# Gates and branch projections with tokens on partitions in a two-layer transformer kernel

## The chip, the cores and the metric

The kernel runs on one core of one Trainium2 chip. Its time is the device time in microseconds (us) of one execution. Beside it stands the span of a profiled execution, which runs from its first to its last instruction.

## The reference, cut to what matters

Two blocks follow one another on 256 tokens of width 2048. Each has a mixer and a feed-forward part. What the change touches is the mixer's gates, its two branch projections and the out projection behind them:

```
z = u @ w_in                                  # u: rms-normed input, 256 x 2048
... , gates = split(z)                        # the last 4096 columns of z
y_a = (first branch: a scan in layer 1, a gated MLP in layer 2)      # 256 x 1024
y_b = (second branch: banded / neighbourhood attention)              # 256 x 1024
gate_a, gate_b = split(sigmoid(gates))        # 256 x 2048 each
merged = gate_a * (y_a @ w_branch_a) + gate_b * (y_b @ w_branch_b)
h = h + merged @ w_out
```

All of it is float32. Layer 2 does the same with `w_in_2`, `w_branch_2` (both halves in one matrix) and `w_out_2`.

## The kernel before, in words

**Products.** Each weight is split into a high and a low float32r part, and so is each operand (`XU` and `XY` hold 16 tiles of 128 features; columns 0 to 255 of a tile are the high parts of the 256 tokens, 256 to 511 the low parts). A product is high*high + high*low + low*high. In `products` the weights are stationary: for each of 8 contraction tiles k of a block, `high(k)` (L432) holds 128x128 of `w_hi` and streams 512 columns of X, and `low(k)` (L437) holds `w_lo` and streams 256. The result has output features on partitions and tokens in the free dimension. In `value_products` and `token_downs` the other layout is used: 128 tokens of X are stationary and 512 columns of a weight chunk stream, three matmuls (L469, L470, L471) for each of two token halves; the result has tokens on partitions.

**The weight stream.** All weights come in blocks of 512 KB in the order in which they are used, by SP, into five slots. ACT rounds block b+4 to `w_hi` (`round_block`, L799), DVE subtracts to get `w_lo` (`low_part`, L1216), and PE multiplies block b. ACT rounds a block only when PE has finished the block that held its slot five blocks earlier (`w_used`). Every engine runs its own straight program in block order, so an ACT step of block b can stand behind a wait for PE's block b.

**The stages in order**, for layer 1: `vals1` (values, tokens on partitions), `heads1` (8 heads of 18 blocks), `branch1` (32 blocks), `out1` (32 blocks), then the feed-forward stages; for layer 2: `gmv`, `heads2` (8 heads of 14 blocks), `branch2`, `out2`, feed-forward. In a head, the first 5 tiles (3 in layer 2) are inputs of the scan or the attention; the last 4 tiles, 8 blocks, are gate columns. A tile takes two blocks (16 contraction tiles). Between blocks PE does small jobs of the scan and the attention (lists `after1`, `after2`). The last jobs of a head in layer 1 stand behind block 17: `attend` (L598, L603) and `scan_rms` (L567).

**What ACT does around the end of a head in layer 1** (step b = 17, then step b = 0 of the next head): it copies the cross half of a finished tile (`copy_cross`, L804), rounds a block, copies the attention's high part (L900), takes Ln and Exp of the scan's norm (L940, L941), waits for two DVE products, copies the result (L943), and then rounds the next block. The next head's step b = 1 has `sigmoid_of` (L880). In layer 2, step b = 0 rounds a block, which needs PE to have finished block 0 of this head, and step b = 1 has a Gelu (L1081).

**Banks.** In `heads1` tile t uses `acc_first` for t = 0 and else `acc[(t-1) % 2]`; in `heads2` the two `acc` banks in turn. A gate tile is summed on DVE (`tile_sum`: bank plus cross), multiplied by `rs` and kept in `G` (L1407, L1580). In the branch stages ACT takes the sigmoid in `G` (L956), and DVE multiplies, adds and forms the low part of the mixed tile (L1436 to L1441), one 128x256 tile at a time, so that the out projection's operand is there with features on partitions.

Of the kernel before, what the change touches and what calls it, by code (L numbers as in the profile page):

```python
# [6 lines left out]
F32 = mybir.dt.float32  # L7
# [32 lines left out]
CHUNK = 512  # L40
OUT_ACT = 3 * D // 8
# [103 lines left out]

def phases():
    plan = [("vals1", 1, 32, 0, 0, None), ("heads1", HEADS, 18, 9, 9, None), ("branch1", 2, 16, 16, 16, None), ("out1", 2, 16, 8, 0, None),
# [3 lines left out]
            ("gmv", 1, 32, 0, 0, None), ("heads2", HEADS, 14, 7, 7, None),  # L151
            ("branch2", 2, 16, 16, 16, None), ("out2", 2, 16, 8, 0, None),
# [21 lines left out]
def two_blocks(  # L174
# [6 lines left out]
    with ExitStack() as ctx:  # L181
# [70 lines left out]
        def head2_bank(i, t):  # L252
            return acc[(7 * i + t) % 2]
# [58 lines left out]
        def gate_of(i, b):  # L312

            j, half = divmod(b, 2)
            return i * 16 + (4 * (j // 2) + 2 * half + j % 2)

        def mixed_before(b, blocks):

            return [b // 2 - 1] if b and b % 2 == 0 else [b // 2] if b == blocks - 1 else []
# [36 lines left out]
        def _(sp):  # L356
# [13 lines left out]
            def side(name, i, b):  # L370
# [6 lines left out]
                if name == "ffn1last" and b == 0:  # L377
# [5 lines left out]
                    sp.wait_ge(S("mz_ready1"), KD)  # L383
                    sp.dma_start(Gf[:, 0:2 * WIDTH],
                                 bass.AP(tensor=norm_rows.tensor, offset=0, ap=[[0, P], [1, 2 * WIDTH]])).then_inc(S("bs_in"), 16)
                if name == "ffn2first" and b == 0:
                    sp.wait_ge(S("mz_ready2"), KD)
                    sp.dma_start(final_row, bass.AP(tensor=norm_rows.tensor, offset=2 * WIDTH, ap=[[0, P], [1, D]])).then_inc(S("bs_in"), 16)
# [30 lines left out]
        def _(pe):  # L419
# [53 lines left out]

            def raw_products(b, banks):
# [49 lines left out]
            def in_tiles(p, i, X, after, bank_of):  # L524
                for b in range(p.blocks):
                    t = b // 2
                    if b % 2 == 0:
                        bank_free(p, i, t)
                    if i == 0 and b in (0, 2):

                        pe.wait_ge(S("vals_out" if p.name == "heads1" else "av_out"), NT * (1 + 2 * (p.name == "heads1") + b // 2))
                    products(p, i, b, bank_of(t), X, KB * (b % 2), b % 2 == 0, b % 2 == 1)
                    for job in after.get(b, []):
                        job(i)
# [91 lines left out]
            for i in range(p.iters):  # L626
                in_tiles(p, i, XU, after1, lambda t: acc_first if t == 0 else acc[(t - 1) % 2])

            def branches(name):

                p = ph[name]
                X = XY if name == "branch1" else XU
                x = name[-1]
                for i in range(p.iters):
                    for b in range(p.blocks):
                        pe.wait_ge(acc_free, p.tile(i, b) - 3 + TILE_CREDIT)
                        if b < 2:

                            pe.wait_ge(acc_free, p.tbase - 1 + b + TILE_CREDIT)
                        if i + b == 0:  # L640

                            pe.wait_ge(S(f"ya_ready{x}"), HEADS - 1)
                            products(p, i, b, four_banks[0], X, 0, True, True, ks=range(KB - 1), used=0)
                        elif i == 0 and b == 1:
                            pe.wait_ge(S(f"yb_ready{x}"), HEADS)
                            products(p, i, b, four_banks[1], X, KB, True, True, used=0)
                            pe.wait_ge(S(f"ya_ready{x}"), HEADS)
                            products(p, i, 0, four_banks[0], X, 0, True, True, ks=(KB - 1,), used=2)
                        else:
                            products(p, i, b, four_banks[b % 4], X, KB * (b % 2), True, True)  # L650

            def out_projection(name):
                p = ph[name]
                X = XU if name == "out1" else XY
                for i in range(p.iters):
                    for b in range(p.blocks):
                        if b % 2 == 0:
                            bank_free(p, i, b // 2)
                        products(p, i, b, acc[b // 2 % 2], X, KB * (b % 2), b % 2 == 0, b % 2 == 1,
                                 operand=one_by_one(S(f"m_ready{name[-1]}"), 0) if b < 2 else None)  # L660
# [103 lines left out]
            for i in range(p.iters):  # L764
                in_tiles(p, i, XY, after2, lambda t: head2_bank(i, t))
# [18 lines left out]
        def _(act):  # L784
# [92 lines left out]

            def sigmoid_of(n, wait_name, done_name, i):
# [24 lines left out]
            for i in range(p.iters):  # L903
                for b in range(p.blocks):
                    t = b // 2
                    if b == 0:
                        round_next(p, i, b)
                    if b % 2:

                        copy_cross(p, i, t, b, acc_first if t == 0 else acc[(t - 1) % 2])  # L910
# [37 lines left out]

            def branches(name, X):
                p, x = ph[name], name[-1]  # L950
                act.wait_ge(S(f"gates_z{x}"), HEADS)
                for i in range(p.iters):
                    for b in range(p.blocks):
                        round_block(p, i, b)
                        gate = G[:, ds(gate_of(i, b), 1), :]
                        act.activation(gate, gate, ACT.Sigmoid).then_inc(S(f"gates_ready{x}"), 1)  # L956
                        free_cross(p, i, b)
                        copy_cross(p, i, b, b, four_banks[b % 4])

                        for j in mixed_before(b, p.blocks):  # L960
                            act.wait_ge(S(f"mz_ready{x}"), i * 8 + j + 1)
                            act.activation(X[:, ds(i * 8 + j, 1), 0:T], work[:, 2 * (j % 2):2 * (j % 2) + 1, 0:T], ACT.Copy)\
                               .then_inc(S(f"mh_ready{x}"), 1)
# [8 lines left out]
            def out_projection(name, X, n0, c0):  # L972
                p = ph[name]
                for i in range(p.iters):
                    for b in range(p.blocks):
                        round_block(p, i, b)
                        if b % 2:
                            j = i * 8 + b // 2
                            operand_tile(n0 * KD + j, X, j, cols[:, ds(j + c0, 1)], p, i, b // 2)
# [3 lines left out]
            out_projection("out1", XY, 0, C_MLP1)  # L983
# [89 lines left out]
            for i in range(p.iters):  # L1073
                for b in range(p.blocks):
                    t = b // 2
                    if b % 2:
                        copy_cross(p, i, t, b, head2_bank(i, t))
                    round_next(p, i, b)
                    if b == 1:
# [16 lines left out]
            out_projection("out2", XU, 2, C_FFN2)  # L1096
# [67 lines left out]
        def _(pool):  # L1164
# [12 lines left out]
            def out_projection(name, n0):  # L1177
                p = ph[name]
                for i in range(p.iters):
                    for b in range(p.blocks):  # L1180
                        if b % 2:
                            add_square(i * 8 + (n0 * KD + b // 2))
# [18 lines left out]
        def _(dve):  # L1201
# [157 lines left out]
            for i in range(p.iters):  # L1359
                for b in range(p.blocks):  # L1360
# [10 lines left out]
                    bank = acc_first if t == 0 else acc[(t - 1) % 2]  # L1371
# [32 lines left out]
                    if b in (11, 13, 15, 17):  # L1404
                        n = (b - 11) // 2
                        tile_sum(p, i, 5 + n, b, 5 + n, bank, wk(8))
                        ins = V.tensor_tensor(G[:, ds(i * 4 + n, 1), :], work[:, 8:9, 0:T],  # L1407
                                              rs[:, :].rearrange("p (a t) -> p a t", a=1), ALU.mult)
                        if n == 3:
                            mark(ins, S("gates_z1"), i + 1)  # L1410
                        else:
                            link(ins)
# [11 lines left out]

            def branches(name, X):
                p, x = ph[name], name[-1]
                for i in range(p.iters):
                    for b in range(p.blocks):
                        low_part(p, i, b)
                        j, half = divmod(b, 2)  # L1430
                        at = 2 * (j % 2)
                        z = work[:, at + half:at + half + 1, 0:T]
# [343 lines left out]
```

## Time and profile before

| | us |
|---|---|
| median of 3 runs | 2780.59 |
| lowest and highest | 2780.02, 2781.06 |
| the profiled execution, its own time | 2781.22 |
| its span | 2779.4 |

The profiled execution's own time is 1.8 us more than its span, and 0.6 us above the median of the runs. Starts in a timeline are us from the start of the span. PE is TensorE's matmuls, PEld its weight loads, which overlap the matmuls. The recorded end of a matmul is modelled and overlaps the next one, so rates are read from starts.

### The profile page before, as it was taken

Reading aid. Unit: us, or ns where it says so; the run is one execution under the profiler, and the core shown is the slowest. Engines: PE = TensorE matmul, PEld = TensorE weight load, DVE = VectorE, ACT = ScalarE, POOL = GpSimd, SP = SyncE. Lnnn points to the kernel's source line nnn. Section 1 sums busy time; section 2 is a strip of 40 time slices with the busy share of each in tenths; the row PEclk is TensorE's granted clock in tenths of the full one; section 3 lists DMA queues with packets and bytes.
Section 4 is the critical chain, followed back from the end, with each engine's and each line's share of the span. In section 5 each row is a group of like instructions: output and inputs, shape, how many; then the busy total and the mean of one; then the engine's idle time right before and its main releaser. Section 6 shows DMA issues by size and latency. Waiting matters only on the chain.

```text
span 2779.4 us, 40598 instructions
## 1 busy us (share of the span) xinstructions
PE 2765.6 (100%) x15440; PEld 2377.4 (86%) x15440; DVE 2075.5 (75%) x3194; ACT 1472.1 (53%) x2184; POOL 63.6 (2%) x72
## 2 busy tenths in 40 slices
PE   9999999999999999999999999999999999999998
PEld 6888888888888888888888888888888888888887
DVE  5687888887677777777786677778778777777776
ACT  5456555565444444444465555556555555555554
POOL 0000000000000000000050000000000000000000
PEclk9999999999999999999999999999999999999999
DMA  7555555555555655555655655655565555555554
GB/s 266 189 172 166 187 173 174 172 190 189 181 193 190 193 184 189 190 191 188 210 197 188 195 180 169 196 175 188 184 203 190 183 192 191 192 190 190 190 189 144
DMA packets 157154, 521.98 MB, mean 188 GB/s; under 512 B 28960, under 2 KB 31392, under 8 KB 156704
## 3 DMA queue, kind: packets, MB, share of 16 engines
q1 hardware_dynamic: 155952, 517.31, 56.5%
q8 instruction: 123, 2.02, 0.3%
q10 hardware_dynamic: 1008, 2.08, 0.2%
q14 instruction: 71, 0.58, 0.1%
HBM read 517.22 MB, written 2.10 MB: 187 GB/s over the span
## 4 chain that ended last, share of the span: by engine, by line
PE 100%; DMA 0%; DVE 0%; ACT 0%; issue 0%; DVEq 0%; SPq 0%
PE acc L432 39%; PE acc L437 19%; PE psT L432 5%; PE psX L432 5%; PE acc_first L432 5%; PE psX L437 3%; PE psT L437 3%; PE acc_first L437 2%; PE acc L469 1%; PE acc L471 1%; PE acc L470 1%; PE psT L715 1%; PE psE L715 1%; PE psE L716 1%; PE psX L717 1%; PE psA L717 1%
## 5 line engine op out<-in xcount | busy, mean ns | idle before, releaser
L1216 DVE TENSOR_TENSOR w_lo<-w_raw,w_hi 128x1024 fp32r<-128x1024 f32 x958 | 1170.3, 1228 | 344.5 <-ACT w_hi L799 315.4
L799 ACT ACTIVATE w_hi<-w_raw 128x1024 fp32r<-128x1024 f32 x958 | 1003.0, 1055 | 553.0 <-PE acc L432 280.3
L432 PE MATMUL acc<-XU,w_hi 128*128 128x512 f32 x2848 | 930.6, 398 | 0.0
L437 PEld LDWEIGHTS acc<-XU,w_lo 128*128 128x128 f32 x2848 | 535.3, 188 | 122.5
L432 PE MATMUL acc<-XY,w_hi 128*128 128x512 f32 x1792 | 576.8, 397 | 0.0
L437 PE MATMUL acc<-XU,w_lo 128*128 128x256 f32 x2848 | 560.0, 278 | 0.0
L432 PEld LDWEIGHTS acc<-XU,w_hi 128*128 128x128 f32 x2848 | 447.8, 189 | 4.1 <-issue 2.7
L437 PEld LDWEIGHTS acc<-XY,w_lo 128*128 128x128 f32 x1792 | 336.7, 188 | 78.3
L437 PE MATMUL acc<-XY,w_lo 128*128 128x256 f32 x1792 | 352.4, 278 | 0.0
L432 PEld LDWEIGHTS acc<-XY,w_hi 128*128 128x128 f32 x1792 | 277.9, 189 | 5.5 <-DVE work L1222 2.7
L804 ACT ACTIVATE cross<-acc 128x256 f32<-128x256 f32 x242 | 92.5, 382 | 335.2 <-PE acc L432 335.2
L432 PE MATMUL acc_first<-XU,w_hi 128*128 128x512 f32 x576 | 188.0, 398 | 0.0
L1222 DVE TENSOR_TENSOR work<-acc,cross 128x256 f32<-128x256 f32 x242 | 102.5, 424 | 105.8 <-ACT cross L804 104.2
L437 PEld LDWEIGHTS acc_first<-XU,w_lo 128*128 128x128 f32 x576 | 108.2, 188 | 25.3
L437 PE MATMUL acc_first<-XU,w_lo 128*128 128x256 f32 x576 | 113.3, 278 | 0.0
L432 PE MATMUL psX<-XU,w_hi 128*128 128x512 f32 x320 | 107.0, 395 | 0.0
L432 PE MATMUL psT<-XU,w_hi 128*128 128x512 f32 x320 | 107.0, 395 | 0.0
L432 PE MATMUL psT<-XY,w_hi 128*128 128x512 f32 x320 | 104.4, 395 | 0.0
L432 PE MATMUL psX<-XY,w_hi 128*128 128x512 f32 x320 | 104.4, 395 | 0.0
L432 PEld LDWEIGHTS acc_first<-XU,w_hi 128*128 128x128 f32 x576 | 90.4, 189 | 0.7
L1167 POOL TENSOR_TENSOR sqacc<-sqacc,sqb 128x256 f32<-128x256 f32 x48 | 43.7, 910 | 1941.0 <-ACT sqb L969 1940.5
L1003 ACT ACTIVATE XU<-work 128x256 fp32r<-128x256 f32 x64 | 26.7, 418 | 98.9 <-DVE work L1482 98.9
(345 smaller groups left out, 3275.9 us busy)
## 6 DMA issues: line engine op xcount, KB each, us to landing
w_raw<-in_weights SPq DMA_DIRECT2D x962, 512.0 KB, 3.4
bias<-in_rel_bias SPq DMA_DIRECT2D x8, 384.0 KB, 3.9
bias<-in_rpb_back SPq DMA_DIRECT2D x32, 96.0 KB, 6.7
hT<-in_x_t SPq DMA_DIRECT2D x8, 256.0 KB, 7.5
G<-in_norm_rows SPq DMA_DIRECT2D x2, 1024.0 KB, 7.3
G<-in_pair_masks ACTq DMA_DIRECT2D x1, 960.0 KB, 5.1
out_dram<-G SPq DMA_DIRECT2D x2, 384.0 KB, 2.5
out_dram<-G ACTq DMA_DIRECT2D x2, 384.0 KB, 3.2
```

Of the source, the lines that this page charges most:

```text
L432: return nc.tensor.matmul(bank[:, :], hi[:, k, col:col + P], X[:, k0 + k, :], start=first and k == 0, stop=last and k == nk - 1 and k % 2 ...
L437: return nc.tensor.matmul(bank[:, 0:T], lo[:, k, col:col + P], X[:, k0 + k, 0:T], start=False, stop=last and k == nk - 1 and k % 2 == 0, s ...
L469: nc.tensor.matmul(bank[:, :], x_hi, hi[:, k, :], start=first, stop=False, skip_group_check=True)
L470: nc.tensor.matmul(bank[:, :], x_hi, lo[:, k, :], start=False, stop=False, skip_group_check=True)
L471: done = nc.tensor.matmul(bank[:, :], x_lo, hi[:, k, :], start=False, stop=last, skip_group_check=True)
L715: nc.tensor.matmul(bank[:, :], x_hi, hi[:, e, :], start=k == 0 and s.group >= 0, stop=False, skip_group_check=True)
L717: done = nc.tensor.matmul(bank[:, :], x_lo, hi[:, e, :], start=False, stop=k == nk - 1, skip_group_check=True)
L799: act.activation(w_hi[s][:, 0:n], w_raw[s][:, 0:n], ACT.Copy).then_inc(hi_done, 1)
L804: act.activation(cross[:, p.cross(i, c) % 2, :], bank[:, T:2 * T], ACT.Copy).then_inc(cross_ready, 1)
L1167: nc.gpsimd.tensor_tensor(sqacc[:, 0, :], sqacc[:, 0, :], sqb[:, 0, :], ALU.add).then_inc(sq_added, 1)
L1216: V.tensor_tensor(w_lo[s][:, 0:n], w_raw[s][:, 0:n], w_hi[s][:, 0:n].bitcast(F32), ALU.subtract).then_inc(lo_ready, 1)
L1222: mark(V.tensor_tensor(dst, bank[:, 0:T], cross[:, p.cross(i, c) % 2, :], ALU.add), acc_free, p.tile(i, t) + 1 + TILE_CREDIT)
```

## The change

The 4 gate tiles of a head, the branch projections and the gating are computed with tokens on partitions:

- A new `token_block` does one block of 2 contraction tiles by 512 weight columns: for each k and each token half three matmuls of 512 columns with X stationary. A head's 8 gate blocks give 256 columns of gate a and 256 of gate b for both token halves, in the banks `acc_first` and `acc[0]`.
- ACT takes the sigmoid straight from those banks with the token's scale (`sigmoid_gates`), two instructions of 128x512 at step b = 0 of the next head, behind `round_next`. PE may write `acc[0]` again, at block 2 of the next head, only when `gates_ready` says that they are done. The DVE sums and products of gate tiles are gone.
- A branch stage is now 4 chunks of 512 columns, 8 blocks each: 4 blocks of y_a into one pair of banks, 4 blocks of y_b into another. DVE multiplies each pair by the gates (`gated`) and adds them.
- The mixed chunk has tokens on partitions, and the out projection needs features there. `turn_chunk` transposes it on PE, 8 transposes of 128x128 for a chunk; ACT copies the high parts (`mixed_high`) and DVE forms the low parts (`mixed_low`), two tiles at once.
- The last chunk is turned inside the out projection, behind its second block. The first four blocks of the out projection are reordered (`out_order`): tile 0 first half, tile 1 first half, then their second halves.
- The weight stream is rearranged to match. Blocks, their number and size stay as they are.

```diff
+NEAR_TILES = {"heads1": 5, "heads2": 3}
+def out_order(i, b):
+    if i == 0 and b < 4:
+        return b % 2, b // 2
+    return b // 2, b % 2
...
+        def head_bank(t):
+            return acc[(t + 1) % 2]
+        gate_banks = [acc_first, acc[0]]
+        branch_banks = [[psT, psX], [acc[1], psA]]
+        turn_banks = [[acc[0], acc_first], [psE, psS]]
...
+            def token_block(p, i, b, X, k0, banks, first, last):
+                ...
+                pe.wait_ge(lo_ready, p.block(i, b) - RAW + 1)
+                for k in range(2):
+                    for a in range(NT):
+                        bank = banks[a]
+                        x_hi, x_lo = (X[:, k0 + k, T * n + a * P:T * n + (a + 1) * P] for n in range(2))
+                        nc.tensor.matmul(bank[:, :], x_hi, hi[:, k, :], start=first and k == 0, stop=False, skip_group_check=True)
+                        nc.tensor.matmul(bank[:, :], x_hi, lo[:, k, :], start=False, stop=False, skip_group_check=True)
+                        done = nc.tensor.matmul(bank[:, :], x_lo, hi[:, k, :], start=False, stop=last and k == 1, skip_group_check=True)
+                done.then_inc(w_used, 1)
...
+            def in_tiles(p, i, X, after):
+                near = NEAR_TILES[p.name]
                 for b in range(p.blocks):
                     t = b // 2
-                    if b % 2 == 0:
-                        bank_free(p, i, t)
+                    if t < near and b % 2 == 0:
+                        if t == 0:
+                            pe.wait_ge(acc_free, p.tile(i, 0) + TILE_CREDIT)
+                        else:
+                            bank_free(p, i, t)
+                        if t == 1:
+                            pe.wait_ge(S(f"gates_ready{p.name[-1]}"), NT * i)
...
+                    if t < near:
+                        products(p, i, b, head_bank(t), X, KB * (b % 2), b % 2 == 0, b % 2 == 1)
+                    else:
+                        if t == near and b % 2 == 0:
+                            pe.wait_ge(acc_free, p.tile(i, near - 2) + 1 + TILE_CREDIT)
+                        k0 = 2 * (b - 2 * near)
+                        token_block(p, i, b, X, k0, gate_banks, k0 == 0, k0 == KD - 2)
...
+            def turn_chunk(x, c):
+                pe.wait_ge(S(f"mixed{x}"), NT * (c + 1))
+                if c >= 2:
+                    pe.wait_ge(S(f"m_ready{x}"), 2 * (c - 1))
+                for n in range(2):
+                    bank = turn_banks[c % 2][n]
+                    for j in range(2):
+                        for a in range(NT):
+                            done = nc.tensor.transpose(...)
+                    done.then_inc(S(f"m_turned{x}"), 1)
...
             def branches(name):          # PE
+                for c in range(p.iters):
+                    for b in range(p.blocks):
+                        ...
+                        token_block(p, c, b, X, k0, branch_banks[kind], b % 4 == 0, b % 4 == 3)
+                        if b == 2 and c:
+                            if c == 1:
+                                pe.wait_ge(S(f"gates_ready{x}"), NT * HEADS)
+                            turn_chunk(x, c - 1)
...
             def out_projection(name):    # PE
+                        products(p, i, b, acc[t % 2], X, KB * half, half == 0, half == 1,
+                                 operand=mixed if i == 0 and b in (0, 2) else None)
+                        if i == 0 and b == 1:
+                            turn_chunk(x, CHUNKS - 1)
...
+            def sigmoid_gates(x, i):     # ACT
+                p, scales = ph[f"heads{x}"], mix_rs if x == 1 else tok_rs
+                act.wait_ge(w_used, p.block(i, p.blocks - 1) + 1)
+                for a in range(NT):
+                    act.activation(head_gates(i, a), gate_banks[a][:, :], ACT.Sigmoid, scale=scales[:, a:a + 1])\
+                       .then_inc(S(f"gates_ready{x}"), 1)
...
                     if b == 0:           # ACT, heads1
                         round_next(p, i, b)
+                        if i:
+                            sigmoid_gates(1, i - 1)
...
                     round_next(p, i, b)  # ACT, heads2
+                    if b == 0 and i:
+                        sigmoid_gates(2, i - 1)
...
+            def mixed_low(x, c, X):      # DVE
+                for n in range(2):
+                    j = 4 * c + 2 * n
+                    dve.wait_ge(S(f"mh_ready{x}"), 2 * c + n + 1)
+                    mark(V.tensor_tensor(X[:, j:j + 2, T:2 * T], turn_tiles(c, n), X[:, j:j + 2, 0:T].bitcast(F32), ALU.subtract),
+                         S(f"m_ready{x}"), 2 * c + n + 1)
+            def gated(x, p, c, kind):
+                dve.wait_ge(w_used, p.block(c, 4 * kind + 3) + 1)
+                dve.wait_ge(S(f"gates_ready{x}"), 2 * NT * (c + 1))
+                for a in range(NT):
+                    gate = chunk_gates(c, a, kind)
+                    mark(V.tensor_tensor(gate, branch_banks[kind][a][:, :].rearrange("p (h n) -> p h n", h=2), gate, ALU.mult),
+                         S(f"branch_read{x}"), NT * (2 * c + kind) + a + 1)
...
-                    if b in (11, 13, 15, 17):
-                        n = (b - 11) // 2
-                        tile_sum(p, i, 5 + n, b, 5 + n, bank, wk(8))
-                        ins = V.tensor_tensor(G[:, ds(i * 4 + n, 1), :], work[:, 8:9, 0:T],
-                                              rs[:, :].rearrange("p (a t) -> p a t", a=1), ALU.mult)
```

## Rows read from the trace of the kernel before

**Rows 1.** The page: span, then busy time and share of each engine

```profile
span 2779.4 us, 40598 instructions
...
PE 2765.6 (100%) x15440; PEld 2377.4 (86%) x15440; DVE 2075.5 (75%) x3194; ACT 1472.1 (53%) x2184; POOL 63.6 (2%) x72
```

**Rows 2.** The waits of PE alone: total us, times, longest

```profile
PE acc L480 <- DMA w_raw<-in_weights: 6.0, 1, 6.0
```

**Rows 3.** Timeline of PE in the first branch stage: start, us, instruction

```profile
571.06 0.39 PE L437 MATMUL psT<-XY,w_lo 128*128 128x256 f32 x2
...
624.00 0.39 PE L437 MATMUL acc<-XY,w_lo 128*128 128x256 f32 x2
```

**Rows 4.** Timeline of PE in `gmv`, tokens on partitions

```profile
1449.63 0.39 PE L469 MATMUL acc<-w_hi,XY 128*128 128x512 f32 x1
...
1454.85 0.39 PE L471 MATMUL acc<-w_hi,XY 128*128 128x512 f32 x1
```

**Rows 5.** Timeline of PE: eight transposes between two blocks of `heads2`

```profile
1568.63 0.60 PE L588 MATMUL psT<-ident,probs 128*128 128x128 f32 x4
1569.07 0.60 PE L588 MATMUL psX<-ident,probs 128*128 128x128 f32 x4
```

**Rows 6.** Timeline of PE from head 0 to head 1 of `heads1`

```profile
155.10 0.43 PE L598 MATMUL psS<-pT,G 128*64 128x256 f32 x1
...
156.25 0.58 PE L432 MATMUL acc_first<-XU,w_hi 128*128 128x512 f32 x1
...
162.03 0.39 PE L432 MATMUL acc<-XU,w_hi 128*128 128x512 f32 x1
```

**Rows 7.** Timeline of ACT over the same stretch; in brackets idle time before

```profile
155.49 1.05 ACT L799 ACTIVATE w_hi<-w_raw 128x1024 fp32r<-128x1024 f32 x1
156.44 0.38 ACT L900 ACTIVATE XY<-psS 128x256 fp32r<-128x256 f32 x1
156.83 1.28 ACT L940 ACT_TABLE_LOAD   x1
...
158.62 1.28 ACT L941 ACT_TABLE_LOAD   x1
159.91 0.42 ACT L941 ACTIVATE work<-work 128x256 f32<-128x256 f32 x1
161.35 0.42 ACT L943 ACTIVATE XY<-work 128x256 fp32r<-128x256 f32 x1 [1.02 <-DVE work L1420]
161.68 1.04 ACT L799 ACTIVATE w_hi<-w_raw 128x1024 fp32r<-128x1024 f32 x1
...
163.96 1.28 ACT L880 ACT_TABLE_LOAD   x1
```

**Rows 8.** The line L830, ACT from a bank with scales: ns min/median/max, first start

```profile
L830 ACT ACTIVATE G<-psA,small x2: 582/636/690, 56.6 to 100.1; 128x512 f32<-128x512 f32 x1, 128x384 f32<-128x384 f32 x1
L830 ACT ACTIVATE G<-psE,small x2: 583/633/683, 57.2 to 100.9; 128x512 f32<-128x512 f32 x1, 128x384 f32<-128x384 f32 x1
```

**Rows 9.** Timeline of ACT at the start of a head of `heads2`

```profile
1579.36 1.06 ACT L799 ACTIVATE w_hi<-w_raw 128x1024 fp32r<-128x1024 f32 x1 [2.47 <-PE acc L432]
1582.09 0.39 ACT L804 ACTIVATE cross<-acc 128x256 f32<-128x256 f32 x1 [1.67 <-PE acc L432]
```

**Rows 10.** Timeline of PE at block 2 of that head

```profile
1581.66 0.63 PE L432 MATMUL acc<-XY,w_hi 128*128 128x512 f32 x2
```

**Rows 11.** Two lines with 128x512 from a bank: DVE L1651, ACT L893

```profile
L1651 DVE TENSOR_TENSOR G<-psT,G x10: 691/691/693, 2230.8 to 2760.8; 128x512 f32<-128x512 f32 x10
L893 ACT ACTIVATE pT<-psT x16: 498/544/591, 152.1 to 1869.4; 128x384 f32<-128x384 f32 x8, 128x512 f32<-128x512 f32 x8
```

**Rows 12.** Windows of PE at the end: length, busy (count), granted clock, DMA

```profile
2771.00:2773.00 2.00, 0.59 (x3) 1.00 1.02 390
...
2775.00:2776.00 1.00, 0.00 (x0) 1.00 0.54 209
2776.00:2777.00 1.00, 0.00 (x0) 0.76 1.03 402
```

More of the change, by code:

```diff
@@ L652, in out_projection @@
[L652 to L660, printed above, removed]
+                            pe.wait_ge(S(f"m_ready{x}"), 2 * (CHUNKS - 1))
@@ L947, in free_cross, with mixed_high @@
                 act.wait_ge(acc_free, p.tile(i, t) - 1 + TILE_CREDIT)
+            def mixed_high(x, c, X):
+                for n in range(2):
+                    j = 4 * c + 2 * n
+                    act.wait_ge(S(f"m_turned{x}"), 2 * c + n + 1)
+                    act.activation(X[:, j:j + 2, 0:T], turn_tiles(c, n), ACT.Copy).then_inc(S(f"mh_ready{x}"), 1)
             def branches(name, X):
-                p, x = ph[name], name[-1]
-                act.wait_ge(S(f"gates_z{x}"), HEADS)
-                for i in range(p.iters):
+                p, x = ph[name], int(name[-1])
+                sigmoid_gates(x, HEADS - 1)
+                for c in range(p.iters):
                     for b in range(p.blocks):
[L954 to L963, printed above, removed]
+                        round_block(p, c, b)
+                        if b == 3 and c:
+                            mixed_high(x, c - 1, X)
             def operand_tile(n, X, j, wcol, p, i, t):
@@ L1370, in _ @@
                     t = b // 2
-                    bank = acc_first if t == 0 else acc[(t - 1) % 2]
+                    bank = head_bank(t)
                     if b == 1:
@@ new lines, in branches @@
+                        low_part(p, c, b)
+                        if b == 3:
+                            gated(x, p, c, 0)
+                            if c:
+                                mixed_low(x, c - 1, X)
+                        if b == 7:
+                            gated(x, p, c, 1)
+                            for a in range(NT):
+                                m = chunk_gates(c, a, 0)
+                                mark(V.tensor_tensor(m, m, chunk_gates(c, a, 1), ALU.add), S(f"mixed{x}"), NT * c + a + 1)
@@ L1462, in out_projection @@
                         low_part(p, i, b)
-                        if b % 2:
-                            j = i * 8 + b // 2
-                            add_to_residual(p, i, b, b // 2, acc[b // 2 % 2], j)
+                        t, half = out_order(i, b)
+                        if i == 0 and b == 1:
+                            mixed_low(name[-1], CHUNKS - 1, M)
+                        if half:
+                            j = i * 8 + t
+                            add_to_residual(p, i, b, t, acc[t % 2], j)
                             low_operand(n0 * KD + j, X, j, cols[:, ds(j + c0, 1)])
+            branches("branch1", XU)
             link(V.tensor_tensor(fm2, cols[:, C_FIN1:C_FIN1 + KD], cols[:, C_MIX2:C_MIX2 + KD], ALU.mult))
-            branches("branch1", XU)
-            out_projection("out1", XY, 0, C_MLP1)
+            out_projection("out1", XU, XY, 0, C_MLP1)
             dve.wait_ge(rs_ready, 2)
@@ L1682, in part, with gates @@
         return w[row:row + ntiles * P, col:col + ncols].reshape(ntiles, P, ncols).transpose(1, 0, 2)
+    def gates(w, row, col):
+        return np.concatenate([part(w, row, 2, col + n * D, HEAD_CHUNK) for n in range(2)], axis=2)
     half = b % 2
@@ L1687, in weight_block @@
         starts = [1, 0, 3, 5, 4]
-        col = starts[t] * WIDTH + i * P if t < 5 else (7 * WIDTH + (t - 5) // 2 * D + (t - 5) % 2 * P + i * (2 * P))
-        return part(a["w_in"][0], half * BLOCK, KB, col)
+        if t >= len(starts):
+            return gates(a["w_in"][0], (b - 2 * len(starts)) * (2 * P), 7 * WIDTH + i * HEAD_CHUNK)
+        return part(a["w_in"][0], half * BLOCK, KB, starts[t] * WIDTH + i * P)
     if name == "vals1":
@@ L1695, in weight_block @@
         starts = [0, 3, 2]
-        col = starts[t] * WIDTH + i * P if t < 3 else (5 * WIDTH + (t - 3) // 2 * D + (t - 3) % 2 * P + i * (2 * P))
-        return part(a["w_in_2"][0], half * BLOCK, KB, col)
+        if t >= len(starts):
+            return gates(a["w_in_2"][0], (b - 2 * len(starts)) * (2 * P), 5 * WIDTH + i * HEAD_CHUNK)
+        return part(a["w_in_2"][0], half * BLOCK, KB, starts[t] * WIDTH + i * P)
     if name == "gmv":
```

143 lines of the change are left out of this document (67 added, 76 removed).

## The prediction, written before the change was run

> **What bounds the kernel now.** I read the page first: PE is busy for 2765.6 of 2779.4 us, DVE for 75% and ACT for 53% of the span [rows 1]. Busy PE alone proves little, since matmul ends are modelled, so I read its waits next: in the whole execution PE waited once, 6.0 us for the first weights, and for nothing afterwards [rows 2]. So every nanosecond taken out of PE's stream shortens the kernel, every one put in lengthens it, and every new wait of PE is paid in full, because there is no idle time for it to hide in. Two questions are left: how many ns PE's stream gains, and whether a new wait binds.
>
> **PE's stream, the part that gets cheaper.** With weights stationary a contraction tile of one 128-column tile costs one 512 and one 256 matmul. In the branch stage the pattern of four matmuls repeats 76 times from 571.06 to 624.00: 52.94 us for 152 such units, 348.3 ns each [rows 3]. With tokens on partitions, 24 matmuls of 512 columns start from 1449.63 to 1454.85, 5.22 us in 23 steps, 227 ns each [rows 4]. For the same work, one k and 512 weight columns on 256 tokens, the old layout takes 4 x 348.3 = 1393 ns and the new one 6 x 227 = 1362 ns. Columns streamed are equal (3072); the gain is 31 ns, from six matmuls in place of eight. How often: 4 gate tiles x 16 k x 8 heads = 512 units a layer, and 16 tiles x 16 k = 256 units a layer in the branches; both layers 1536 units, 384 groups of four. 384 x 31 = 12 us less (11 to 13).
>
> **PE's stream, the part that is added.** 8 transposes for each chunk, 4 chunks, 2 layers: 64. The attention has the same instruction, 128x128 of float32 against `ident`: four of them start in 0.44 us [rows 5], so a chunk costs 0.87 us and all eight chunks 7.0 us more. Net of both: 5 us less. That would be the result if no wait bound.
>
> **The new wait in layer 1.** PE's block 2 of a head writes `acc[0]` and now waits until ACT has taken the sigmoid of the previous head's gates out of it. ACT issues these two instructions at its step b = 0, behind everything of step b = 17. Take head 0 to head 1. PE's block 17 ends near 155.1, its jobs follow, block 0 of head 1 starts at 156.25 and block 2 at 162.03 [rows 6]. ACT meanwhile rounds a block, copies the attention, loads a table and takes Ln, loads a table and takes Exp, waits 1.02 us for DVE's two products, copies, and rounds again: that ends at 161.68 + 1.04 = 162.72 [rows 7]. Before the change nothing of PE stood behind this chain. Now the gates do: the sigmoid's table, which is loaded later at 163.96, moves ahead of them (1.28), and the two instructions follow, 128x512 from a bank with a scale; L830 has that shape at 0.69 us, the second starting 0.6 after the first [rows 8]. 162.72 + 1.28 + 0.6 + 0.69 = 165.3. One term falls away: the cross copy of the last gate tile is gone, so that the round at 155.49 starts 0.28 earlier and the chain with it: 165.0, and some 0.06 for the semaphore. PE, ready at 162.03, waits 3.06 us. Bounds: 2.9 if ACT's instructions close up more, 3.4 if the 0.28 isn't gained and a weight load (0.19, which is otherwise hidden) comes on top. I take 3.2. Head 0 has no predecessor: 7 heads, 22.4 us (20 to 24). PE's next blocks don't catch it up, since PE had no slack; the next head meets the same chain again.
>
> **The new wait in layer 2.** There is no long chain, but ACT's step b = 0 rounds a block first, and that waits for PE's block 0 of the new head. It ran from 1579.36 to 1580.42 [rows 9]. Then come the sigmoid's table, not loaded here before (the sets of Exp and Gelu alternate), and both instructions: 1580.42 + 1.28 + 0.6 + 0.69 + 0.06 = 1583.1. PE's block 2 started with the second matmul of the row at 1581.66, at 1581.89 [rows 10]. So PE waits 1.2 us; with a part of the weight load 1.3, 7 times, 9.1 us (7 to 11).
>
> **What lies beside other work.** DVE loses 64 sums and 64 products in the heads, ACT 64 cross copies and 64 sigmoids: nothing of PE waited for them [rows 2], so they are worth nothing, and the cover they give back isn't needed. In a chunk of 8 blocks (8 x 12 x 227 ns = 21.8 us) DVE has 8 subtractions of about 1.2 and eight operations of 128x512 at 0.69 [rows 11], 15.4 us in all; ACT has less. The turn of chunk c-1 stands behind the third block of chunk c, 8.2 us after the last product, while DVE needs 4 x 0.69 = 2.8 us and their semaphores: hidden. The branch banks are freed at least 7 us before PE writes them again. The start of a branch stage now needs the last head's y_a at block 3 and not in the middle of block 1, so it gets more room. In the out projection the last chunk is turned behind block 1; the first k that needs it comes 4 x 348 = 1.4 us after the transposes. Its path is half of the transposes (0.6 with the drain), a copy of at most 0.59 and a subtraction of 0.69 [rows 11], and three semaphores, 2.1 us after the turn began against 0.87 + 1.39 = 2.26; the second pair arrives at 2.8 against 2.96. Hidden by some 0.15 us; if not, each layer pays up to 0.5. I take nothing. The stream of weights (512 KB in 2.72 and not in 2.79 us) stays hidden, for PE never waited for one. SP's queue has the same issues in the same order.
>
> **The sum**, against the profiled execution's own time: 2781.2 - 12 + 7 + 22.4 + 9.1 = 2807.7. That execution lies 0.6 above the median of the runs, so I predict **2807 us**, 26 us or 0.95% slower. 0.2% (5.6 us) is about what a measurement of this kernel can tell from no change.
>
> **The rivals.**
>
> *The gates come in time (faster).* ACT would have to deliver them before block 2, in layer 1 some 3.2 us and in layer 2 some 1.3 us sooner. Then 2780.6 - 5 = 2775.5. It decides where the 14 waits together fall below 5 us, 0.36 us each. For it: ACT is idle for half of the span [rows 1], and table loads, 1.28 us each, come where the compiler puts them. Against it: ACT works in order, and the three loads and the wait for DVE stand between two points that PE fixes.
>
> *One table load fewer.* If Ln and Exp of the scan's norm shared one set, ACT's chain would lose 1.28 us in 7 heads, 2807 - 9 = 2798. The rows show two loads, at 156.83 and at 158.62 [rows 7], and nothing in the edit touches them. The Trainium skill ("ScalarE: Activation LUTs", section on table sets) says that Ln followed by Exp needs one load, as one set has both; by that rule this rival is the result, and the trace disagrees: it shows one load for each of the two.
>
> *The clock falls in the wait.* If the granted clock went to half during each wait of layer 1 and stayed there after it as long as it here takes to fall, seven times 2 to 2.5 us would be added: 2823. Against it: after the last matmul, at 2771.6, the clock was still full from 2775 to 2776 and fell within 2776 to 2777 [rows 12], over 4 us later, and the wait is 3. The two levels there are 2.4 and 1.2 GHz. The Trainium skill ("TensorE: Matmul & The Clock Gate", section "Why this matters for your kernels") warns against idle gaps between bursts of matmuls, as the clock then goes back to the lower level; by that warning the 7 long waits are at risk.
>
> *More waits than two kinds.* The out projection's first operands, a later Gelu or a late round after the stall might bind too: up to 0.5 us in each head and 1 us in each stage, 2812 to 2818.
>
> *Only layer 1 waits.* If ACT could round late and take the gates first in layer 2, or the table stayed, 2807 - 9 = 2798.
>
> **Chances.** Both waits as worked out, 2800 to 2813: 0.70. One load fewer 0.03, only layer 1 0.04, more waits 0.08, clock 0.06, gates in time or some gain of PE that I don't see 0.09. The range of 2795 to 2818 holds the first four, 0.85 less what their own ends leave out. Slower by over 0.2%: all but the last, and a part lost to error, 0.88; faster 0.10; within 0.2% 0.02.
>
> **What the profile of the changed kernel would show.** PE's waits would list a matmul of block 2 (L432 in the new numbering) released by ACT's sigmoid, 14 times, about 3.1 us each in layer 1 and 1.2 in layer 2. PE's busy time would fall by some 5 us. Gate and branch blocks would show matmuls 227 ns apart. ACT's timeline would show a table load right behind the second round of the chain and then the two sigmoids. The chain that ended last would name ACT and DVE beside PE, for the first time. I am wrong if PE's waits don't name the sigmoid, if the waits are much shorter than 3.1 and 1.2, or if the granted clock leaves 1.0 between 160 and 560.

## The result, and the profile after

The changed kernel takes 2818.87 us (median of 4 runs, 2817.76 to 2819.44) against 2780.61 for the kernel before, run beside it: ratio 1.0138, 95% interval 1.0126 to 1.0150. It is 38 us slower. I forecast 26 us slower, 2807 in a range of 2795 to 2818; the direction was right, the time lies 0.9 us above the range.

First the page of the changed kernel, head and part 1, which answer to [rows 1]:

```profile
span 2815.9 us, 38435 instructions
...
PE 2773.4 (98%) x14736; PEld 2353.3 (84%) x14736; DVE 1987.1 (71%) x2938; ACT 1445.8 (51%) x2015; POOL 63.6 (2%) x72
```

PE's busy time went up by 8 us where its stream was to become 5 shorter, and 29 us of idle time are new: 42.5 us of the span are not busy now, 13.8 were before. The waits of PE, which answer to [rows 2], say where most of that is:

```profile
PE acc L449 <- issue: 28.4, 14, 3.0
PE acc L512 <- DMA w_raw<-in_weights: 6.3, 1, 6.3
```

14 waits at a product into `acc` (L449 is the old L432), the longest 3.0 us. They stand under "issue": the view names no releaser for them, so the timelines have to find it. PE from head 0 to head 1 of layer 1, the answer to [rows 6]:

```profile
160.42 0.40 PE L449 MATMUL acc<-XU,w_hi 128*128 128x512 f32 x1
163.81 0.77 PE L449 MATMUL acc<-XU,w_hi 128*128 128x512 f32 x1 [2.99 <-issue]
164.37 0.63 PE L454 MATMUL acc<-XU,w_lo 128*128 128x256 f32 x2
164.80 1.05 PE L449 MATMUL acc<-XU,w_hi 128*128 128x512 f32 x2
165.65 0.63 PE L454 MATMUL acc<-XU,w_lo 128*128 128x256 f32 x2
166.08 1.05 PE L449 MATMUL acc<-XU,w_hi 128*128 128x512 f32 x2
```

and ACT over the same stretch, the answer to [rows 7]:

```profile
153.89 1.06 ACT L866 ACTIVATE w_hi<-w_raw 128x1024 fp32r<-128x1024 f32 x1 [1.27 <-PE acc L503]
...
155.24 1.28 ACT L1017 ACT_TABLE_LOAD   x1
156.53 0.47 ACT L1017 ACTIVATE work<-psE,small 128x256 f32<-128x256 f32 x1
157.03 1.28 ACT L1018 ACT_TABLE_LOAD   x1
...
160.09 1.04 ACT L866 ACTIVATE w_hi<-w_raw 128x1024 fp32r<-128x1024 f32 x1
161.15 1.28 ACT L949 ACT_TABLE_LOAD   x1
162.44 0.69 ACT L949 ACTIVATE G<-acc_first,small 128x512 f32<-128x512 f32 x1
163.03 0.68 ACT L949 ACTIVATE G<-acc,small 128x512 f32<-128x512 f32 x1
```

The second sigmoid (L949) ends at 163.71, PE's product starts at 163.81. From 160.42 to 163.81 are 3.39 us where 0.23 is normal: a wait of 3.15 us, seven times alike. In layer 2 the same distance is 1.44 us, a wait of 1.2, seven times (once 1.3).

Then there is what the waits don't show. In the last rows of PE's timeline two products take 1.05 us, where two took 0.63 in [rows 10], and a pattern of four matmuls takes 1.28 us, from 164.80 to 166.08, where 2 x 0.348 = 0.70 is normal. Windows of PE (length, busy, granted clock, DMA share, GB/s) say why:

```profile
163.80:169.60 5.80, 5.79 (x18) 0.50 0.68 236
169.60:222.00 52.40, 52.40 (x284) 1.00 0.46 159
222.00:226.00 4.00, 1.01 (x6) 1.00 0.13 49
...
285.50:289.10 3.60, 3.60 (x13) 0.53 0.78 249
...
347.00:350.50 3.50, 3.50 (x13) 0.51 0.63 200
...
408.50:412.00 3.50, 3.50 (x13) 0.51 0.77 243
...
470.00:473.40 3.40, 3.40 (x13) 0.50 0.67 254
```

After the wait of head 1 the granted clock is half, 1.2 GHz, until 169.6; behind it the four matmuls take 0.70 us again. Heads 3, 4, 5 and 6 have such a stretch of 3.4 us, and it begins 0.3 to 1.5 us after the wait, when PE is already at work again (in head 3 PE is back at 285.38 and the low stretch begins at 285.7). So nearly all of it is paid for. Heads 2 and 7 have the same wait and keep the full clock; what sets them apart from the other five, no run here shows. That is the rival to which I gave 0.06.

The heads themselves show what a low stretch costs. From the first product of a head to that of the next, heads 2 and 7 take 59.46 and 59.45 us, heads 3 to 6 take 61.00 to 61.05, and head 1 takes 62.11. That is 1.54 to 1.59 us for each short stretch and 2.65 for the long one, 8.9 us in all.

To see the sizes I took the length of each stage from all traces, from the start of its first product to that of the next stage's (us; `vals1` from the start of the span). The columns behind the first two are the experiments of the next section: early1 and both take the gates early in layer 1 and in both layers, one set loads one table set for Ln and Exp, fill and longer fill the wait and lengthen it, late set and between have the set behind the gates and the gates between Exp and DVE's products, and twice issues the transposes twice.

```
              before  changed  early1  both   one set  fill   longer  late set  between  twice
vals1          99.95   98.86  100.38   99.67   99.23   98.48   99.10   99.16    99.15    99.64
heads1        451.86  481.15  461.27  461.23  458.53  472.11  494.29  452.33   449.56   449.65
branch1        89.38   89.99   89.99   89.99   89.99   89.99   89.99   89.99    89.99    92.61
out1           89.17   90.05   90.06   90.06   90.06   90.06   90.06   90.06    90.06    90.93
heads2        342.54  347.87  347.89  338.76  347.71  347.71  347.77  338.76   338.76   338.76
branch2        89.29   89.93   89.93   89.93   89.93   89.93   89.93   89.93    89.93    92.55
out2           89.17   90.06   90.06   90.06   90.06   90.06   90.06   90.06    90.06    90.93
```

All other stages are equal within 0.02 us. `vals1` differs from execution to execution by up to 1.9 us with no pattern. The changed kernel loses 29.3 us in `heads1`, 5.3 in `heads2` and 3.0 in the branch and out stages.

### The profile page after: what moved, and what is told of

It reads as the page before. It is cut to its first block, busy times and chain, and to the rows that moved or that the text cites. A ratio compares the mean times of both kernels' runs of the same rounds, so it can differ in the third digit from the quotient of the medians.

```text
span 2815.9 us, 38435 instructions
## 1 busy us (share of the span) xinstructions
PE 2773.4 (98%) x14736; PEld 2353.3 (84%) x14736; DVE 1987.1 (71%) x2938; ACT 1445.8 (51%) x2015; POOL 63.6 (2%) x72
## 4 chain that ended last, share of the span: by engine, by line
PE 98%; issue 1%; DMA 0%; DVE 0%; ACT 0%; DVEq 0%; SPq 0%
PE acc L449 29%; PE acc L454 14%; PE psX L449 4%; PE psT L449 4%; PE acc_first L449 4%; PE acc L501 3%; PE acc L503 3%; PE acc L502 3%; PE acc_first L501 2%; PE psT L454 2%; PE psX L454 2%; PE acc_first L503 2%; PE acc_first L502 2%; PE acc_first L454 2%; PE acc L488 1%
## 5 line engine op out<-in xcount | busy, mean ns | idle before, releaser
L449 PE MATMUL acc<-XU,w_hi 128*128 128x512 f32 x2336 | 766.6, 400 | 20.9 <-issue 20.9
L454 PEld LDWEIGHTS acc<-XU,w_lo 128*128 128x128 f32 x2336 | 443.4, 190 | 103.1
L454 PE MATMUL acc<-XU,w_lo 128*128 128x256 f32 x2336 | 462.8, 280 | 0.0
L449 PEld LDWEIGHTS acc<-XU,w_hi 128*128 128x128 f32 x2336 | 369.6, 191 | 24.1 <-issue 23.0
L449 PE MATMUL acc<-XY,w_hi 128*128 128x512 f32 x1152 | 371.0, 397 | 7.5 <-issue 7.5
L454 PEld LDWEIGHTS acc<-XY,w_lo 128*128 128x128 f32 x1152 | 216.4, 188 | 50.4
L454 PE MATMUL acc<-XY,w_lo 128*128 128x256 f32 x1152 | 226.5, 278 | 0.0
L449 PEld LDWEIGHTS acc<-XY,w_hi 128*128 128x128 f32 x1152 | 178.9, 189 | 12.3 <-issue 12.2
L449 PE MATMUL acc_first<-XU,w_hi 128*128 128x512 f32 x448 | 145.2, 395 | 0.0
L1305 DVE TENSOR_TENSOR work<-acc,cross 128x256 f32<-128x256 f32 x154 | 65.4, 425 | 106.1 <-ACT cross L871 105.2
L449 PE MATMUL psX<-XU,w_hi 128*128 128x512 f32 x256 | 85.6, 395 | 0.0
L449 PE MATMUL psT<-XU,w_hi 128*128 128x512 f32 x256 | 85.6, 395 | 0.0
L449 PE MATMUL psX<-XY,w_hi 128*128 128x512 f32 x256 | 83.0, 395 | 0.0
L449 PE MATMUL psT<-XY,w_hi 128*128 128x512 f32 x256 | 83.0, 395 | 0.0
L449 PEld LDWEIGHTS acc_first<-XU,w_hi 128*128 128x128 f32 x448 | 70.3, 189 | 0.5
```

Of the source, the lines that this page charges most:

```text
L449: return nc.tensor.matmul(bank[:, :], hi[:, k, col:col + P], X[:, k0 + k, :], start=first and k == 0, stop=last and k == nk - 1 and k % 2 ...
L454: return nc.tensor.matmul(bank[:, 0:T], lo[:, k, col:col + P], X[:, k0 + k, 0:T], start=False, stop=last and k == nk - 1 and k % 2 == 0, s ...
L1305: mark(V.tensor_tensor(dst, bank[:, 0:T], cross[:, p.cross(i, c) % 2, :], ALU.add), acc_free, p.tile(i, t) + 1 + TILE_CREDIT)
```

## The experiments

My theory: the waits for the gates cost 7 x 3.15 + 7 x 1.2, and in layer 1 they bring the clock down, some 8 us more. The rivals: PE's new blocks or transposes are slow in themselves; the low clock costs nothing of its own; something else waits behind the gates. The ratios below are to the kernel before, run again beside each experiment (2780.18 or 2780.49 us).

**The gates of layer 1 early.** ACT takes them at its own step b = 17 and not at the next head's b = 0.

```diff
@@ ACT, heads1, b == 17
+                        if i < HEADS - 1:
+                            sigmoid_gates(1, i)
                         high_of_attention(1, i, XY)
@@ ACT, heads1, b == 0
-                        if i:
-                            sigmoid_gates(1, i - 1)
```

> Layer 1 alone: ACT takes the sigmoid of a head's gates right behind the round of its own step b = 17, ahead of the attention copy and of Ln and Exp; layer 2 as in the changed kernel. Theory (the two waits of 3.15 and 1.2 us, and a granted clock that falls in some of the long ones): the seven long waits of PE go, and with them the half clock; PE's waits list only seven of about 1.2 us, and the time is 2818.9 - 7 x 3.23 - 8 = 2788. Rival (the clock or PE's token blocks are slow for another reason, not for the waits): the waits go but low stretches or 8 us stay, 2796.

Measured: 2798.55 us, ratio 1.0064 (1.0049 to 1.0079). The seven long waits are gone and the granted clock is 1.0 throughout the heads, but it is 10 us slower than I expected. Its waits of PE:

```profile
PE psA L588 <- DVE HS L1367: 9.5, 7, 1.4
PE acc L449 <- issue: 7.5, 7, 1.2
```

A new wait has come, 1.4 us in each of seven heads by the view and 1.52 from start to start: L588 is the first level product of the scan, behind block 5. 7 x 1.52 = 10.6 us is what my theory lacks. The time is nearer to the rival's 2796, but the rival is not right: no low stretch is left, and the 10 us stand in a wait that neither of the two had.

**Both layers early.** As above, and in layer 2:

```diff
@@ ACT, heads2
-                    round_next(p, i, b)
                     if b == 0 and i:
                         sigmoid_gates(2, i - 1)
+                    round_next(p, i, b)
```

> The same in layer 1, and in layer 2 the sigmoid ahead of the round of step b = 0. Theory: no wait of PE is left but the first, and the time is that of PE's stream: 2780.6 + 7.0 for the transposes - 9 to 12 for the cheaper blocks = 2776 to 2779, faster than both kernels. Rival (something hidden behind the waits, such as the later next head on ACT and DVE, is exposed when they go): new waits of 0.5 us or more in each head, 2782 or more.

Measured: 2789.00 us, ratio 1.0032 (1.0019 to 1.0044). Layer 2 is as the theory has it: `heads2` takes 338.76, 3.8 less than before the change. In layer 1 the rival is right, a wait appears when another goes. ACT's timeline of this run shows how:

```profile
158.66 1.28 ACT L1017 ACT_TABLE_LOAD   x1
...
160.45 1.28 ACT L1018 ACT_TABLE_LOAD   x1
...
163.51 1.05 ACT L866 ACTIVATE w_hi<-w_raw 128x1024 fp32r<-128x1024 f32 x1
...
165.79 1.28 ACT L954 ACT_TABLE_LOAD   x1
167.35 0.42 ACT L954 ACTIVATE work<-work 128x256 f32<-128x256 f32 x1 [0.28 <-DVE work L1311]
```

The sigmoid's table is loaded for the gates, thrown out for Ln, then for Exp, and loaded again for the next head's forget gate (L954). With 4 loads in the chain that sigmoid starts at 167.35, 11.6 us after the head's first product (155.71); in the changed kernel it started at 164.93, 10.1 us after it (154.88), PE waiting meanwhile. The scan's chain on DVE hangs on it and ends at L588.

**One table set for Ln and Exp.** The gates stay late.

```diff
@@ ACT, heads1, b == 16
-                        if i == HEADS - 1:
-                            act.preload_act_table_set("natural_log_exp_and_others")
+                        act.preload_act_table_set("natural_log_exp_and_others")
```

> Only the table of ACT changes: the set that holds both Ln and Exp is loaded at step b = 16 of every head of layer 1, not of the last alone; the sigmoid stays at step b = 0 of the next head. Theory: two loads of 1.28 us leave the chain between PE's block 17 and the gates, so the waits of layer 1 shrink from 3.15 to 0.6 us (7 x 2.55 = 18 us), and the clock no longer falls (8 us): 2818.9 - 26 = 2793, with low stretches gone. Rival (the chain is set by something else than the loads, such as DVE's products): waits above 1.5 us, 2800 or more.

Measured: 2795.92 us, ratio 1.0056 (1.0042 to 1.0070). Its waits of PE are 14, none above 1.1 us by the view:

```profile
PE acc L449 <- issue: 14.7, 14, 1.1
```

From start to start they are 1.21 us in both layers. So the wait lost 1.94 us a head and not 2.55. What stays is the other bound, the one of layer 2: the round of step b = 0 needs PE's block 0. ACT's timeline shows it idle before that round:

```profile
158.50 1.06 ACT L866 ACTIVATE w_hi<-w_raw 128x1024 fp32r<-128x1024 f32 x1 [0.49 <-PE acc L449]
159.58 1.28 ACT L949 ACT_TABLE_LOAD   x1
```

The clock is full in all heads. `heads1` is 22.6 us shorter than in the changed kernel, 7 x 1.94 = 13.6 of it wait and the other 9.0 the clock.

**The wait filled.** The same wait, with PE busy in it.

```diff
@@ PE, in_tiles, b == 2
+                        if t == 1 and i and p.name == "heads1":
+                            for _ in range(13):
+                                nc.tensor.matmul(psT[:, :], XU[:, 0, 0:P], XU[:, 1, :], start=True, stop=True)
                         if t == 1:
                             pe.wait_ge(S(f"gates_ready{p.name[-1]}"), NT * i)
```

> The waits stay as long as they are, but in layer 1 PE fills each with 13 matmuls of 512 columns into a bank that nobody reads (2.95 us), so that it is busy while it would wait. Theory (the low clock comes from the idle time): the clock stays at 1.0 and the time falls by the cost of the low stretches alone, 2818.9 - 8 = 2811; ACT's gates come when they came before. Rival (the low clock costs nothing or has another cause): 2819 to 2820.

Measured: 2808.79 us, 10 us less than the changed kernel, by 91 more matmuls. PE's timeline shows the filling in the place of the wait:

```profile
160.27 3.11 PE L567 MATMUL psT<-XU 128*128 128x512 f32 x13
163.38 0.50 PE L449 MATMUL acc<-XU,w_hi 128*128 128x512 f32 x1
163.72 0.40 PE L454 MATMUL acc<-XU,w_lo 128*128 128x256 f32 x2
```

From the product at 160.03 to the one at 163.38 are 3.35 us, as in the changed kernel (3.39), so ACT's side is untouched, and windows of 6 us behind the wait show a granted clock of 1.00 in each of the seven heads. A head takes 59.43 to 59.47 us, as long as heads 2 and 7 of the changed kernel, which kept the full clock: the filling itself neither saves nor costs time. `heads1` is 9.0 us shorter, so the low clock costs 9.0, and idle time of PE brings it about. The rival that it costs nothing falls.

**The wait made longer.**

```diff
@@ ACT, heads1, b == 0
                         if i:
+                            for _ in range(2):
+                                link(act.activation(probs[:, 0, :, :], probs[:, 1, :, :], ACT.Copy))
                             sigmoid_gates(1, i - 1)
```

> The changed kernel with the waits of layer 1 made longer: ACT copies 128x512 twice, each with a wait for itself, ahead of the gates in heads 1 to 7, about 1.3 us. Theory (a longer wait puts the clock down in more heads): 7 x 1.3 = 9 us of wait more and low stretches in all 7 heads and not 4, 3 to 8 us more: 2831 to 2836. Rival (the falls are chance and don't go with the length): 9 us more and again about 4 falls, 2828.

Measured: 2830.95 us, ratio 1.0181 (1.0165 to 1.0196), at the lower edge of the theory. (The expectation speaks of 4 falls in the changed kernel; the trace has 5.) Each wait is now 4.34 us, and the clock falls behind all seven (columns as above):

```profile
163.70:170.50 6.80, 5.27 (x17) 0.50 0.62 220
228.60:232.00 3.40, 3.40 (x12) 0.50 0.43 146
290.00:293.40 3.40, 2.88 (x9) 0.51 0.55 187
351.50:358.30 6.80, 5.77 (x18) 0.50 0.58 198
```

and so at 416.3, 477.8 and 539.2. Three of the seven stretches are 6.8 us. `heads1` grew by 13.1 us over the changed kernel, 8.3 by the waits themselves and 4.8 by the clock.

**The early gates with one load less.** The run at 2789.00 with the one set for Ln and Exp loaded behind the gates (`preload_act_table_set` after `high_of_attention`).

> The gates early in both layers, as in the run at 2789.0, but the one table set for Ln and Exp is loaded behind the gates: one load of 1.28 us less in ACT's chain. Theory (the new wait of 1.5 us at L588 is ACT's chain arriving late at the next head's first sigmoid): the wait shrinks by 1.28 to about 0.2 us, 7 times, 2789.0 - 9 = 2780. Rival (the wait comes from DVE's own queue of work, which the tables don't touch): it stays above 1 us, 2786 or more.

Measured: 2780.38 us, ratio 0.9998 (0.9989 to 1.0007). L588 starts 0.48 us behind the product before it and no longer 1.75 us: the wait fell by 1.27 us, the length of the load. So the wait at L588 was ACT's chain, arriving late by its table loads; DVE's own queue, which this edit doesn't touch, would have kept the wait.

**The gates between Exp and DVE's products.** The one set is loaded at step b = 16, and the gates fill ACT's wait for DVE; layer 2 as in the run with both layers early.

```diff
@@ ACT, heads1, b == 16: one set in every head, as above
@@ ACT, heads1, b == 17
                         act.activation(wk(5), wk(5), ACT.Exp, scale=-0.5).then_inc(S("o_rstd"), 1)
+                        if i < HEADS - 1:
+                            sigmoid_gates(1, i)
                         act.wait_ge(S("ya_z1"), i + 1)
```

> Layer 1: one table set for Ln and Exp, loaded at step b = 16 of every head, and the gates' sigmoid between Exp and the wait for DVE's products; layer 2 as in the run before (sigmoid ahead of the round). Theory: the gates are ready about 5 us after block 17 (needed at 7), and ACT's later steps come no later than in the kernel before, so neither the gates nor the scan's first product is waited for. Time: 2780.2 + 3.0 for branches and out projections - 3.8 for heads2 - 2.4 for heads1 = 2777, just faster than both. Rival (moving the gates forward always delays the next head's forget gate, whatever the tables): waits at L588 of 0.5 us or more remain, 2781 or more.

Measured: 2777.42 us (2776.85 to 2778.26), ratio 0.9988 (0.9980 to 0.9997): faster than the changed kernel by 41 us and than the kernel before by 3. ACT and then PE's waits:

```profile
155.55 0.47 ACT L1014 ACTIVATE work<-psE,small 128x256 f32<-128x256 f32 x1
156.06 0.42 ACT L1015 ACTIVATE work<-work 128x256 f32<-128x256 f32 x1
156.49 1.28 ACT L949 ACT_TABLE_LOAD   x1
157.79 0.69 ACT L949 ACTIVATE G<-acc_first,small 128x512 f32<-128x512 f32 x1
158.37 0.68 ACT L949 ACTIVATE G<-acc,small 128x512 f32<-128x512 f32 x1
158.94 0.42 ACT L1019 ACTIVATE XY<-work 128x256 fp32r<-128x256 f32 x1
```

```profile
PE acc L512 <- DMA w_raw<-in_weights: 5.6, 1, 5.6
```

The two norm instructions follow one another with no load between, the gates are done at 159.05, and the table stays for the next head's sigmoids. PE again waits for nothing but the first weights, and `heads1` is 2.8 us shorter than in the run before.

**The transposes twice.** The last kernel with every transpose of `turn_chunk` issued twice into the same place (`for j in (0, 0, 1, 1)`).

> The same as the first of this call, but each transpose of the mixed chunks is issued twice into the same place: 128 in place of 64. Theory (a transpose costs PE 109 ns and nothing else): 64 x 0.109 = 7.0 us more than its twin, 0.87 for each chunk, in the windows of the branches 2.6 and of the out projections 0.9. In the out projection the longer turn pushes the first operand back too, so that 0.1 to 0.5 us of wait may come there. Rival (the transposes are partly hidden behind weight loads): clearly under 7.

Measured: 2784.93 us in one run. By the table each branch stage grew by 2.62 us and each out projection by 0.87, 6.98 together: 109 ns a transpose, none of it hidden, and no wait in the out projection even with a turn of twice the length.

## Why the prediction was wrong, point by point

1. **PE is the bound and every wait is paid in full**: right. PE's waits went from 1 to 15, and the stages without new waits or transposes kept their length to 0.02 us.
2. **The wait in layer 1**: right. Forecast 3.06 and with a part of the weight load 3.2; measured 3.15, and the distance from the product behind the wait to its `low` is 0.31 in head 2's case against 0.235 in the steady stream, 0.07 more. ACT's chain was right to 0.1 us, the 0.28 of the missing cross copy included. By the letter one of my signs of being wrong came here: the view of waits does not name the sigmoid. The timelines do, as the second sigmoid ends 0.10 us before PE's product.
3. **The wait in layer 2**: right. Forecast 1.2 and 1.3 with the load; measured 1.2.
4. **The transposes**: right. 7.0 forecast, 6.98 by the doubling.
5. **The cheaper blocks**: the term was too large. The kernel without waits has all of it: `heads2` fell by 3.8, `heads1` by 2.3, and the branches, less 3 turns of 0.87 each, by 2.0 each. That is 10.1 and not 12. `heads1` is short by 1.7 us, and the traces say in which blocks. In head 3 the three gate blocks with no job of the scan or the attention between them take 8.27 us (kernel with the gates between, from 366.46) against 8.45 before (from 368.47), 0.06 a block less as forecast. The other five stand with jobs before and behind them, and gain 0.09 together where 0.31 was forecast: 0.22 us short in a head, 1.8 in eight. One piece of it: in the token layout a matmul ahead of a level product into `psA` (255.51 to 255.85 in the changed kernel) takes 0.34, in the old layout 0.26. Whether that is a weight load or a product of DVE that has just not come was not tried.
6. **What lies beside other work**: right for the branch stages, the out projections and the weight stream; in none of them is there a wait.
7. **The step that failed: that the granted clock stays full in a wait of 3 us.** I took it from [rows 12], where it fell over 4 us after the last matmul. That was one fall, and it said nothing about how soon another may come. It cost 9 us: 9.0 by the filled wait, 9.0 by the waits shortened with one table set, 8.9 by the lengths of the changed kernel's own heads. The stretches themselves agree: 6.8 us in head 1, of which 1.0 still lay in the wait, and four of 3.4 are 19.5 us of work, in which four matmuls took 1.28 us and not 0.70, so that 46% of it, 8.9 us, is lost. With 9 for the clock and 2 for point 5 my 2807 becomes 2818; the kernel took 2819. The rival was named with its place; its price, 2 to 2.5 us in all seven heads, is in the runs 1.5 to 1.6 in four heads, 2.65 in one and nothing in two. The clock alone would have given 2816, inside my range; that would have been luck, for the upper end of the range was meant for other waits and not for the clock.
8. **The rival of one table load fewer**: its rule, that Ln followed by Exp needs one load (the Trainium skill, "ScalarE: Activation LUTs", section on table sets), holds here only where the kernel asks for that set. The kernel before already did so in its last head, and its trace shows it: one load at 549.53 (L936), then Ln at 552.20 and Exp at 552.70 with none between. I had not used these times, and they show that an edit can choose the set. Left to itself, the program loads a set for each, at 155.24 and 157.03 in the changed kernel, so as a forecast the rule was wrong. Asked for at step b = 16, where ACT has time, neither load is left in the chain, and the changed kernel gets 23 us faster by that edit alone, 13.6 of it wait and 9.0 the clock. ACT in the last head of the kernel before:

```profile
549.53 1.28 ACT L936 ACT_TABLE_LOAD   x1
...
552.20 0.47 ACT L940 ACTIVATE work<-psE,small 128x256 f32<-128x256 f32 x1 [0.24 <-PE psE L567]
552.70 0.42 ACT L941 ACTIVATE work<-work 128x256 f32<-128x256 f32 x1
```

The low clock agrees with the warning of the Trainium skill ("TensorE: Matmul & The Clock Gate", section "Why this matters for your kernels") against idle gaps between bursts of matmuls. I had the warning and set one row against it.

## What to carry to other kernels

When PE has no idle time, a bank that one more engine must read is a new point of order: follow that engine's program from the last product to the read, with every table load and every wait in between, for that is what PE will wait for. A wait of PE can cost more than its length, since the clock may be down behind it: here 3.15 us of wait brought 1.5 to 2.7 us more in five heads of seven. A single late fall in a trace is no proof that it won't be. Moving the read forward moves something else back; the place that costs nothing is where the engine already waits for another, here between Exp and DVE's products.

## What the runs showed of the hardware

- The granted clock after idle time of PE, in these heads: waits of 1.2 to 1.5 us, 56 of them in the changed kernel and five of the experiments, and no fall; waits of 3.15 us, a fall in 5 heads of 7; waits of 4.34 us, 7 of 7. With the 3.15 us filled by matmuls, none in 7.
- The low clock in the rows: a pattern of four float32r matmuls, two of 512 columns and two of 256, took 1.28 us at 1.2 GHz and 0.70 at 2.4.
- A table load took 1.28 us, and where the next instruction waited for nothing else, it started 11 or 12 ns behind it.
- In PE's stream a float32r matmul of 512 columns costs 227 ns with the tokens stationary; with the weights stationary one of 512 and one of 256 columns cost 348 ns together. A float32 transpose of 128x128 costs 109 ns, about half a 512-column matmul.
